# All the probability-value products of a head pair at one step, in four attentions of a two-block network

## The reference, cut to what matters

```
s = q @ k.T * scale (+ mask or bias)
p = softmax(s [, sink])
o = p @ v
```

## Time and profile before

| | us |
|---|---|
| three runs | 2131.64, 2136.08, 2538.79; median 2136.08 |
| profiled execution, its own time | 2130.91 |
| span of its profile | 2129.0 |
| attention A, 219.7 to 400.5 | 180.8 |
| attention B, 580.0 to 785.0 | 205.0 |
| attention E, 995.6 to 1047.0 | 51.4 |
| attention O, 1607.8 to 1701.0 | 93.2 |
| mean granted TensorE clock | 0.98 of 2.4 GHz |

### The profile page before, as it was taken

How to read it: one execution, slowest core, us unless ns; L and a number is a source line. 1 busy time by engine, 2 the same in 40 slices (tenths; PEclk the granted TensorE clock), 3 DMA queues, 4 the chain that set the end, 5 groups by cost and what they waited for, 6 DMA issues and landing times.

```text
span 2129.0 us, 28194 instructions
## 1 busy us (share of the span) xinstructions
PE 2009.5 (94%) x10600; PEld 1569.0 (74%) x10600; DVE 997.8 (47%) x1774; ACT 882.3 (41%) x1668; POOL 698.8 (33%) x394
## 2 busy tenths in 40 slices
PE   5999999999999999998899999999998899999998
PEld 3888655688665567887677888887885477888886
DVE  3520778523376653378436435343116625525254
ACT  4322667423376654535553222235225643323233
POOL 1322122342100045331234444443442334444433
PEclk9999999999999999998899999999999999999999
DMA  8222333132100013231124433332332122333332
GB/s 297 60 67 63 100 100 109 51 106 59 44 1 1 1 30 88 62 97 33 40 82 149 135 95 89 105 92 75 109 97 60 45 78 80 109 98 93 100 92 85
DMA packets 209467, 174.36 MB, mean 82 GB/s; under 512 B 6080, under 2 KB 180775, under 8 KB 208183
## 3 DMA queue, kind: packets, MB, share of 16 engines
q1 hardware_dynamic: 206096, 163.86, 25.4%
q0 software_dynamic: 2192, 8.45, 1.2%
q10 hardware_dynamic: 1047, 0.26, 0.1%
HBM read 170.41 MB, written 7.38 MB: 84 GB/s over the span
## 4 chain that ended last, share of the span: by engine, by line
PE 43%; issue 4%; ACT 2%; DVE 2%; POOL 2%; POOLq 0%; DVEq 0%; ACTq 0%
PE ps L369 13%; PE ps L371 13%; PE ps L370 13%; PE ps L737 1%; POOL WL L1563 1%; PE ps L701 1%; PE ps L599 1%; ACT PB L653 0%; ACT TMP L514 0%; PE ps L682 0%; DVE PB L641 0%; PE ps L618 0%; DVE XC L2549 0%; PE ps L448 0%; POOL YT L1551 0%
## 5 line engine op out<-in xcount | busy, mean ns | idle before, releaser
L1563 POOL TENSOR_TENSOR WL<-raww,WH 128x1024 fp32r<-128x1024 f32 (+1 forms) x247 | 583.2, 2366 | 910.1 <-ACT WH L321 901.1
L369 PE MATMUL ps<-HH,WH 128*128 128x512 f32 (+1 forms) x1368 | 523.2, 382 | 16.5 <-DVE HL L2529 7.8
L370 PE MATMUL ps<-HL,WH 128*128 128x512 f32 (+1 forms) x1368 | 519.1, 379 | 0.0
L371 PE MATMUL ps<-HH,WL 128*128 128x512 f32 (+1 forms) x1368 | 518.5, 379 | 0.0
L321 ACT ACTIVATE WH<-raww 128x1024 fp32r<-128x1024 f32 (+1 forms) x247 | 254.7, 1036 | 412.1 <-PE ps L371 408.8
L369 PEld LDWEIGHTS ps<-HH,WH 128*128 128x128 f32 x1368 | 259.6, 190 | 73.8 <-issue 17.8
L371 PEld LDWEIGHTS ps<-HH,WL 128*128 128x128 f32 x1368 | 259.6, 190 | 48.5
L370 PEld LDWEIGHTS ps<-HL,WH 128*128 128x128 f32 x1368 | 260.0, 190 | 46.7
L701 PE MATMUL ps<-ident,PB 128*128 128x128 f32 x952 | 157.5, 283 | 24.5 <-ACT PB L653 16.0
L653 ACT ACTIVATE PB<-PB,NB 128x512 f32<-128x512 f32 (+3 forms) x192 | 116.5, 607 | 72.7 <-DVE NB L641 69.8
L701 PEld LDWEIGHTS ps<-ident,PB 128*128 128x128 f32 x952 | 109.5, 142 | 50.2 <-ACT PB L653 26.9
(11 more groups left out here) (346 smaller groups left out, 3113.4 us busy)
## 6 DMA issues: line engine op xcount, KB each, us to landing
raww<-in_ffn_w_up SPq DMA_DIRECT2D x88, 512.0 KB, 3.8
raww<-in_ffn_w_down SPq DMA_DIRECT2D x40, 512.0 KB, 3.3
raww<-in_ada_w SPq DMA_DIRECT2D x32, 512.0 KB, 3.6
raww<-in_odd_w_in SPq DMA_DIRECT2D x24, 512.0 KB, 3.8
raww<-in_a_w_in SPq DMA_DIRECT2D x20, 512.0 KB, 3.8
raww<-in_even_w_in SPq DMA_DIRECT2D x17, 512.0 KB, 3.9
ADA<-in_ada_w SPq DMA_DIRECT2D x6, 1024.0 KB, 16.5
raww<-in_b_w_in SPq DMA_DIRECT2D x12, 512.0 KB, 3.8
```

The source lines that it names most:

```text
L369: nc.tensor.matmul(out, lh, rh, start=start and k == ks[0], stop=False)
L370: nc.tensor.matmul(out, lh, rl, start=False, stop=False)
L371: ins = nc.tensor.matmul(out, ll, rh, start=False, stop=stop and k == ks[-1])
L1563: nc.gpsimd.tensor_tensor(lo, raw_slot(k), hi.bitcast(F32), ALU.subtract).then_inc(*split_lo.mark(k))
```

## The change

The number of steps over which a pair's products are spread becomes 1 everywhere; where they begin stays. So latent pairs of A and all pairs of B, E and O do all their products at z + 3 and their output at z + 4 (before: z + 3 to z + 6, and z + 7); context pairs of A at z + 5 and z + 6 (before: z + 5, z + 6, and z + 7). The last pair of each attention was so already. In E and O the default plan holds, as in B.

```diff
--- before.py
+++ after.py
@@ -878,7 +878,7 @@
             jobs = A["jobs"]
             A.setdefault("pt", lambda r: ((r + 1) % 3, 0))
             A.setdefault("pt_free", lambda r: (r - 3) | 1)
-            A.setdefault("pv_plan", lambda r: (3, 4))
+            A.setdefault("pv_plan", lambda r: (3, 1))
             if A.get("paired"):
                 A["seq"] = [(r + h, i) for r in range(0, len(jobs), 2) for i in range(NT) for h in range(2)]
             else:
@@ -1113,7 +1113,7 @@
                                       "fill_pe": a_fill_pe, "fill_dve": a_fill_dve, "per": 4, "gate": a_gate,
                                       "pt": lambda r: ((0, 0), (2, 0), (1, 0), (1, C))[r % 4],
                                       "pt_free": lambda r: (r - 4) | 1,
-                                      "pv_plan": lambda r: (3, 4) if r % 4 == 1 else (5, 2),
+                                      "pv_plan": lambda r: (3, 1) if r % 4 == 1 else (5, 1),
                                       "bc": BCA, "bc_free": lambda r: gated["A", r],
                                       "q": a_q, "k": a_k, "q2": a_q2, "kh": a_kh, "kl": a_kl}))
 
```

## The result

| | before | after |
|---|---|---|
| median | 2134.35 us (4 runs) | 2151.14 us (4 runs, 2150.34 to 2151.81) |
| span of the profile | 2129.0 | 2149.8 |
| mean granted clock | 0.980 | 0.969 |

The ratio is 1.0085, 95% interval 1.0069 to 1.0100: the change costs 17 us by the medians and 18 by the ratio, which leaves out one slow run of the kernel before (2538.79), where 8 were forecast to be gained. It lies past the end of the range (2145).

A forecast was written before the change was run, and what follows sets the result against it. TensorE, busy 2009.5 of 2129.0 us, was taken as the bound. B -9, A -3, E +1 and O +3.5 sum to -7.5 us, taking the median from 2136.1 to 2128.6, called 2128; range 2115 to 2145.

The forecast's parts named there:

- the output's move: B: output multiplication from z+7 to z+4 ends most waits for the next queries' low parts, about 0.9 us per pair.
- the pieces: All attentions: each piece of products costs TensorE some 0.15 us extra; 82 fewer save 12.3 us, in B 0.45 per pair.
- But 2.9 us of products are gone from exactly these steps, so TensorE is where it was by z+9.: A: scores of z+7 and z+8 come about 1 us late, but the 2.9 us of products moved away make that good.
- Together 4.0 of 4.3: it just fits: A: VectorE loses 2.5 us in the gathered products and 1.5 at the output, within its 4.3 us idle per period.
- the -3: A in all: 8 periods at -0.4 us each, ends -0.6 and +1.5 per period.
- Rival 1: At z+4 the output multiplication blocks VectorE, waiting for gate or copy: +10 in sum, 2146 us; A 8 x 1.0; chance 0.20.
- rival 3: The granted clock falls: E and O +18 on the forecast, 2146 us, or all 32 pairs +58, 2186; chance 0.07.
- O's term: O: period from 10.72 to 11.2 us, +0.5 (ends -0.4, +1.5), over 7 pairs +3.5 us.
- +1: E in all: 3 pairs at +0.4 us a period, ends -0.6 and +1.5.
- The tests set beforehand: Wrong if B's period doesn't fall by 1 us, A's grows over 0.5, or the granted clock in O's middle is under 1.

The follow-up runs named there:

- be_pad: Kernel before with the products of B and E in one go, and unread transposes where TensorE waits in E and O: 2114.61 us, ratio 0.9915.

## Why the prediction was wrong

**B was right.** From the first spread to the seventh it took 158.2 us before (609.44 to 767.62) and 148.5 after (633.14 to 781.60): 1.6 less in each of six periods, where 1.3 was forecast. By the sum the size is right, but not by its terms. The waits for b_ql fell from 6.8 to 4.4, not to nearly nothing, so the output's move gave 2.4 of the 6.3 us set on it (7 x 0.9), and the run with late output has B at 204.9, only 1.9 above 203.0. The lump itself gave the 7.9 before that: TensorE's busy time in B fell from 197.0 to 191.5, by 5.5 where 3.2 (7 x 0.45) were set down for the pieces. Over the whole program it rose, from 2009.5 to 2014.7, where 10 less were forecast: in A and O, where the clock fell, it is 5.0 and 7.6 more.

**A failed at one sentence**: "But 2.9 us of products are gone from exactly these steps, so TensorE is where it was by z+9." The stands behind "Together 4.0 of 4.3: it just fits" were sized well: 2.5 and 1.5 us were forecast, 3.02 and 1.39 measured in the period shown. What was wrong is that idle time of a whole period can take them up. VectorE's idle 4.3 us are waits for scores and fillers spread over twelve steps, each bound to TensorE two tiles ahead; a stand at z+4 delays the maximum of z+5 and with it the scores of z+7. In the period shown VectorE is idle for 8.3 us: 4.4 in the two stands and still 3.9 elsewhere, where the same period had 4.9 before. So hardly more than 1 of the 4.4 us was taken up. That the scores of z+7, being late, give VectorE its next work late too is argued from this, not shown; the rate is shown: of 3.7 us of delay 1.75 stay at the full clock and 2.6 at the clock it had. In the place of the -3 stands +22.3, 18.0 in the seven periods and 4.2 behind the last lump, where nothing had been set down. Rival 1 had the place and the sign. It was to decide from 0.3 us over VectorE's slack; 4.4 of 4.3 are 0.1 over, and it decided all the same. Its price for A, +8, was a third of what came, as it too paid only for what did not fit the slack.

**The clock failed as a step that I left out.** I held it at 1.00 in A and O, since periods with waits of 1 us had it there, and gave rival 3, which saw it fall in E and O or further, a chance of 0.07. In A it is now 0.93 and costs at least 6.8 us; in O, where +0.5 a period was forecast, the period at 0.96 is 11.33, near the 11.2 of the forecast, and the one at 0.74 is 14.21. At like clock one go costs O 3.6 us (93.5 against 89.9), where +3.5 were forecast. So O's term was right at the full clock, and what was missing is that its lumps would run at half of it. A lump takes 4.11 us in the one period and 2.37 in the other, 1.7 of the 2.9 between them, and VectorE stands 3.4 us for the spread's copy ahead of each output (24.0 in seven), not 1.9. Rows of the kernel after:

```profile
1641.40 4.11 PE L737 MATMUL ps<-o_pt,ARENA 128*64 128x512 f32 x16
...
1668.67 2.37 PE L737 MATMUL ps<-o_pt,ARENA 128*64 128x512 f32 x16
```

The row that should have weighed more was there: the last pair's lump at a granted 0.50. The Trainium skill (TensorE: Matmul & The Clock Gate, A second HAM failure mode) names brief idling between groups as a cause of swings between the two levels. By that rule this change would lose in A and O; the traces of the changed kernel and the run with unread transposes agree with it (clock 0.93 and 0.85, and 1.00 and 0.98 with the waits filled).

**E**: -2.0 for +1, within the ends given. The run be_pad shows that near the full clock its plan makes no difference that can be told, and E with its old plan moved by as much between runs (54.6 and 57.2), so the difference is probably the clock's (0.72 before, 0.75 after).

**The tests set beforehand** did their work: A's period was to grow by no more than 0.5 and grew by 2.6 in the mean, and the granted clock in O's middle was to be 1 and is 0.74 and 0.96 in the two periods shown. B's period was to fall by 1 us and did.

## What to carry to other kernels

Don't pay for a delay out of an engine's idle time over a period: where two engines run two tiles apart, look for the first instruction that the other side waits for, and count the delay from there, here at half its size at the full clock and 0.7 with the clock that came. Price the granted clock with every change that gathers TensorE's work or bares its steps, and where the clock is under 1, try unread products in the waits: here they brought 9 us in E and O together. And a plan of this kind belongs to each loop by itself: one go was right in B, where VectorE has 8 of 26 us to spare and no clock was lost, and wrong in A and O.

## What was not expected of the hardware

A wait of 2.05 us in a loop that is else dense was followed by a stretch partly at half the clock (1.00, then 0.75 in the next 6.9 us; windows of the kernel after, before and behind the wait's end). It is not so each time: the periods of A with waits of 1.39 and 1.44 us stayed at 1.00, the one with 1.29 was at 0.93.

```profile
288.77:294.20 5.43, 3.38 (x30) 2.55 (x29) 3.04 (x7) 1.78 (x6) 2.99 (x3) 1.00 0.32 96
294.20:301.07 6.87, 6.20 (x37) 4.20 (x37) 5.18 (x15) 4.62 (x13) 1.62 (x2) 0.75 0.09 11
```

The second is a price of the late output. In that run VectorE's subtraction L830, 0.95 us by itself, took 2.07 when it began 0.02 us behind GpSimd's gate product, as long as both one after the other, less 0.16. GpSimd, then VectorE, in the run with late output:

```profile
290.29 1.28 POOL L809 TENSOR_TENSOR ARENA<-ARENA,BCA 128x512 f32<-128x512 f32 x1 [8.34 <-ACT BCA L690]
```

```profile
290.31 2.07 DVE L830 TENSOR_TENSOR a_q<-ARENA,a_q 64x768 fp32r<-64x768 f32 x1
```

It recurs, in four of seven periods in all (2.07 or 2.08, begun 0.02 or 0.03 us behind), with 1.25 to 1.31 in the others, begun some 0.8 us behind. The Trainium skill (SBUF — State Buffer, Who interferes with whom) says that a VectorE instruction with two SBUF inputs contends with a GpSimd instruction that reads SBUF, since its second input comes through a read interface that the two share; L830 and L809 are such a pair, and these rows agree. In the changed kernel the early output kept the two apart, as VectorE was waiting for that very product (L830 0.95 each time): some of what the late output won in A it paid here.
